# A hybrid decoder layer on eight cores: weights cast to bf16 once and reloaded from a device-memory scratch

## Chip, cores and metric

One Trainium2 chip, all 8 cores. The batch of 16 sequences is split, two sequences per core; the cores run the same program on their own data and do not exchange anything. The metric is the device time in microseconds of the slowest core, taken as the median over several runs.

## The reference

One decoder layer over x of shape (16, 4096, 1024), all in float32:

```python
xn = rms_norm(h, mix_norm)
z = xn @ w_in                               # 3 x 512 conv columns, 3 x 512 q/k/v, 8 forget gates
y_conv = gate_b * causal_depthwise_conv(gate_c * u, conv_w)
y_attn = forgetting_attention(q, k, v, log_sigmoid(z[..., o_f:] + b_f))   # 8 heads x 64, causal
y = group_rms_norm(concatenate([y_conv, y_attn]), mix_out_norm)
h = h + y @ w_o
g, up = split(rms_norm(h, ffn_norm) @ w_gate_up)                          # 2 x 2816
h = h + (silu(g) * up) @ w_down
h = h + sigmoid(rms_norm(h, ple_norm) @ w_ple_gate + b_ple_gate) * (p @ w_ple_proj)
return rms_norm(h, final_norm)
```

The weights are the same for all tokens.

## The kernel before

Each core walks its two sequences in blocks of 512 tokens: 8 blocks a sequence, 16 blocks in all (block 0 to block 15 in this text). A block is computed from end to end before the next: projections and short convolution, attention over all keys of the sequence so far, output projection, feed-forward, the gated input embedding (gate part, L857), final norm. The work grows within a sequence, because attention covers more keys. Activations stay in SBUF as four float32 tiles of 128 tokens (`h_0` to `h_3`), in two sets that alternate from block to block.

Every block streams all weights anew. They are packed on the host into 31 groups (`wpack`, float32) in the order in which a block uses them: 6 for the input projection (0 to 5: q, k, v, b, c, u), 3 for the output projection, then for each of two halves of the feed-forward the gate/up groups (6, then 5) and 4 down groups, 2 for the gate and 1 for the embedding's projection (28 to 30). In bf16 20 of them have 1 MiB, 4 have 0.75, 4 have 0.625 and 3 have 0.5: 27 MiB per block. `issue_group` (L375) loads one group from `wpack` into one of four bf16 slots in SBUF (`wslot`); the transfer is issued on GpSimd's queue (POOL) and casts from float32 to bf16 on the way. `wget` and `wrel` (L394, L399) drive it: group i goes into slot i % 4, and is issued as soon as the program has released group i - 4, that is, behind TensorE's last read of that slot. The first four loads are chained by a buffer `Bchain`: each waits until the one before it has landed.

Everything else that is moved goes on SyncE's queue (SP): the x tiles of the next block at the top of a block (`load_x`, L424), the four p tiles of the block (L751; two buffers, so tiles 2 and 3 wait for the cast of tiles 0 and 1 at L753), and the four y tiles at its end (L890). The x load of a tile waits for the y store of the same tile, since both use the same `h` buffer.

Order on each queue is the program's order; a helper class `Prog` records the operations, derives waits from the buffers that each reads and writes, and emits them per engine. A transfer that waits holds up what stands behind it on its engine.

Other lines that are named below: L477 transposes the normalised tile on TensorE and L484 (VectorE) writes it as `xnT`; L492 is the common projection (input, gate/up); L543 the v projection; L767 to L777 the output projection, added to `h` at L783; L817 the down projection; L836 the transposes of p, copied to `pT` by VectorE at L840, which L863 needs in the same step as L857.

Of the kernel before, what the change touches and what calls it, by code (L numbers as in the profile page):

```python
# [7 lines left out]
BF16 = mybir.dt.bfloat16  # L8
# [137 lines left out]
def block_groups():  # L146
    specs = []

    def wspec(kind, **kw):
        d = dict(kind=kind)  # L150
        d.update(kw)
        specs.append(d)
        return len(specs) - 1

    d = {}
    d["win"] = {nm: wspec("cols", w="w_in", c0=512 * j) for nm, j in
                (("q", 3), ("k", 4), ("v", 5), ("b", 0), ("c", 1), ("u", 2))}
    d["woc"] = wspec("rows", w="w_o", r0=0, n=4, c0=0, ncol=1024)
    d["woa"] = [wspec("rows", w="w_o", r0=512, n=4, c0=512 * dh, ncol=512) for dh in range(2)]
    d["ffn"] = []  # L160
    for (f_lo, f_n) in ((0, 12), (12, 10)):
        gu = [wspec("gu", f0=(f_lo + 2 * j) * 128) for j in range(f_n // 2)]
        dn = []
        n1 = f_n // 2
        for dh in range(2):
            a = wspec("rows", w="w_dn", r0=f_lo * 128, n=n1, c0=512 * dh, ncol=512)
            b = wspec("rows", w="w_dn", r0=(f_lo + n1) * 128, n=f_n - n1, c0=512 * dh, ncol=512)
            dn.append((a, b, n1, f_n - n1))
        d["ffn"].append((f_lo, f_n, gu, dn))
    d["pg"] = [wspec("cols", w="w_pg", c0=512 * dh) for dh in range(2)]  # L170
    d["pp"] = wspec("rows", w="w_pp", r0=0, n=2, c0=0, ncol=1024)
    return specs, d

def group_len(g):
    return g["n"] * g["ncol"] if g["kind"] == "rows" else 4096
# [22 lines left out]
def build(nc, nblk=8, nseq=SEQ_PER_CORE):  # L198
    P = Prog()
    es = ExitStack()  # L200

    def dram(name, shape, kind="ExternalInput"):
        return nc.dram_tensor(name, list(shape), F32, kind=kind).ap()

    x_d = dram("x", [SEQ_PER_CORE, S, D])
    p_d = dram("p", [SEQ_PER_CORE, S, 256])
    bspecs, bplan = block_groups()
    NG = len(bspecs)
    wpack_d = dram("wpack", [NG, 128, 4096])
    wf_d = dram("wf", [128, 64])  # L210
    gpc_d = dram("gpc", [128, 24])
    gconv_d = dram("gconv", [128, 4])
# [14 lines left out]
    y_d = dram("y", [SEQ_PER_CORE, S, D], kind="ExternalOutput")  # L227

    def sb(name, shape, dt):
        return es.enter_context(nc.sbuf_tensor(name, list(shape), dt))  # L230
# [62 lines left out]
    hT = [[sb(f"h{b}_{t}", [128, D], F32) for t in range(4)] for b in range(2)]  # L293
# [40 lines left out]
    pin = [sb(f"pin{i}", [128, 256], F32) for i in range(2)]  # L334
# [5 lines left out]
    NSLOT = 4  # L340
    wslot = [sb(f"wslot{i}", [128, 4096], BF16) for i in range(NSLOT)]
    Bslot = [Buf() for _ in range(NSLOT)]
# [29 lines left out]
    Bchain = Buf()  # L372
    Bchain.w = Bc_pool.w

    def issue_group(i):  # L375
        g = bspecs[i % NG]
        s_ = i % NSLOT
        n = group_len(g)
        o = wslot[s_][:, 0:n]
        i_ = wpack_d[i % NG, :, 0:n]  # L380
        wr = [Bslot[s_], Bchain] if i < NSLOT else [Bslot[s_]]
        P.dma("pool", lambda e, o=o, i_=i_: e.dma_start(out=o, in_=i_), f"w{s_}", writes=wr)  # L382

    released = set()

    def wpump():
        while wstate["issued"] < NGROUPS:
            j = wstate["issued"]
            if j >= NSLOT and (j - NSLOT) not in released:
                break  # L390
            issue_group(j)
            wstate["issued"] += 1
# [19 lines left out]
    for gb in range(nseq * nblk):  # L412
        off = gb * NG
        d = {}
# [9 lines left out]
    def load_x(sq, blk, hb):  # L424
        for tt in range(4):
            r0 = blk * T + tt * 128
            P.dma("sp", lambda e, o=hT[hb][tt][:], i_=x_d[sq, r0:r0 + 128, :]: e.dma_start(out=o, in_=i_),
                  f"h{hb}_{tt}", writes=[Bh[hb][tt]])

    def rstd_all(hb):  # L430
# [68 lines left out]

    gblk = 0  # L500
    load_x(0, 0, 0)
    for sq in range(nseq):
        for blk in range(nblk):
            hb = gblk % 2
# [3 lines left out]
            if nxt < nseq * nblk:  # L508
                load_x(nxt // nblk, nxt % nblk, nxt % 2)
# [8 lines left out]
            for hp in range(4):  # L518
# [4 lines left out]
                     reads=[Bps[b]], writes=[BQT[2 * hp]])  # L523
                P.op("act", lambda e, b=b, hp=hp: e.activation(out=QT[64:128, 2 * hp + 1, :], in_=PS[b][64:128, :],
                                                                func=AF.Copy, scale=0.125),
                     reads=[Bps[b]], writes=[BQT[2 * hp + 1]])
            wrel(pl["win"]["q"])
            sK, BK = wget(pl["win"]["k"])
            for hp in range(4):
# [3 lines left out]
                     reads=[Bps[b]], writes=[BKT[hp]])  # L533
# [55 lines left out]
            def ftr(e, bx=bx, blk=blk):  # L589
                ins = None  # L590
                for tt in range(4):
# [5 lines left out]
                 reads=[Bps[bx]], writes=[Bcrow])  # L597
# [105 lines left out]
            for i in range(len(units) + LOOK):  # L703
                if i < len(units):
                    h, kt, c0, dg, first, last = units[i]
                    hp, s_ = h // 2, h % 2
# [5 lines left out]
                    def fqk(e, sbk=sbk, hp=hp, rows=rows, kt=kt, c0=c0, dg=dg, h=h):  # L712
# [10 lines left out]
                        out=Pb[pi][:, c0:T], in_=PS[sbk][:, c0:T], func=AF.Exp, bias=cK[:, kt, h:h + 1], scale=1.0),  # L723
                        reads=[Bps[sbk], BcK], writes=[BP[pi]])
                j = i - LOOK
                if j >= 0:
                    h, kt, c0, dg, first, last = units[j]
                    if first:
# [5 lines left out]
                        reads=[BP[pi], BVA], writes=[Bps[ob]])  # L734
                    if last:
                        P.op("act", lambda e, ob=ob: e.activation(out=osq[0:65, :], in_=PS[ob][0:65, :],  # L736
                                                                   func=AF.Square),
                             reads=[Bps[ob]], writes=[Bosq])
# [9 lines left out]

            for tt in range(4):
                r0 = q0 + tt * 128  # L750
                P.dma("sp", lambda e, o=pin[tt % 2][:], i_=p_d[sq, r0:r0 + 128, :]: e.dma_start(out=o, in_=i_),  # L751
                      f"pin{tt % 2}", writes=[Bpin[tt % 2]])
                P.op("dve", lambda e, tt=tt: e.tensor_copy(out=pbf[:, tt, :], in_=pin[tt % 2][:]),  # L753
                     reads=[Bpin[tt % 2]], writes=[Bpbf[tt]])
# [4 lines left out]
            for tt in range(4):  # L759
                for dh in range(2):  # L760
# [14 lines left out]
                    def fo2(e, b=b, tt=tt, wav=wav):  # L775
# [8 lines left out]
                        out=hh[:, dh * 512:(dh + 1) * 512], in0=hh[:, dh * 512:(dh + 1) * 512], in1=PS[b][:],  # L784
# [4 lines left out]
            for (f_lo, f_n, gu, dn) in pl["ffn"]:  # L789
                for j in range(f_n):  # L790
# [7 lines left out]
                         reads=[Bps[bg]], writes=[Bsg[si]])  # L798
                    P.op("dve", lambda e, bu=bu, si=si, j=j: e.tensor_tensor(out=actT[:, j, :], in0=sg[si][:],  # L799
                                                                              in1=PS[bu][:], op=ALU.mult),  # L800
                         reads=[Bsg[si], Bps[bu]], writes=[BactT[j]])
                    if j % 2 == 1:
                        wrel(gu[j // 2])
                for dh in range(2):
# [5 lines left out]
                    for tt in range(4):  # L810
                        b = bank()

                        def fd(e, b=b, tt=tt, av=av, bv_=bv_, na=na, nb=nb):
# [9 lines left out]
                            out=hh[:, dh * 512:(dh + 1) * 512], in0=hh[:, dh * 512:(dh + 1) * 512], in1=PS[b][:],  # L823
# [7 lines left out]
            def ftp(e, pbv=pbv):  # L831
                ins = None
                for pc in range(2):
# [7 lines left out]
                 reads=[Bps[tb]], writes=[BpT])  # L841
# [4 lines left out]
            for dh in range(2):  # L846
# [5 lines left out]
                for tt in range(4):  # L852
                    bgt, bpp = bank(), bank()

                    def fg(e, bgt=bgt, bpp=bpp, tt=tt, dh=dh, pgv=pgv, ppv=ppv):
# [6 lines left out]
                        for pc in range(2):  # L862
# [5 lines left out]
                         reads=[Bps[bgt]], writes=[Bacc])  # L868
                    P.op("dve", lambda e, bpp=bpp: e.tensor_tensor(out=acc[:], in0=acc[:], in1=PS[bpp][:],  # L869
                                                                    op=ALU.mult),  # L870
                         reads=[Bps[bpp]], writes=[Bacc])
                    hh = hT[hb][tt]
                    P.op("dve", lambda e, hh=hh, dh=dh: e.tensor_tensor(
                        out=hh[:, dh * 512:(dh + 1) * 512], in0=hh[:, dh * 512:(dh + 1) * 512], in1=acc[:],
# [8 lines left out]
            for tt in range(4):  # L883
                h = hT[hb][tt]
                P.op("dve", lambda e, h=h, tt=tt: e.scalar_tensor_tensor(out=h[:], in0=h[:],
                                                                          scalar=stat[:, 8 + tt:9 + tt],
                                                                          in1=gfin[:], op0=ALU.mult, op1=ALU.mult),
                     reads=[Bstat[tt], Bconst], writes=[Bh[hb][tt]])
                r0 = q0 + tt * 128
                P.dma("sp", lambda e, h=h, o=y_d[sq, r0:r0 + 128, :]: e.dma_start(out=o, in_=h[:]),  # L890
                      f"h{hb}_{tt}", reads=[Bh[hb][tt]])
            gblk += 1

# [70 lines left out]
```

How the kernel before makes its waits and increments, by code:

```python
        def run(engname, eng, final=False):  # L106
            waited = {}
            idx = 0
            for fn, deps, dsem in self.q[engname]:
                for (k, v) in deps:
                    if waited.get(k, 0) < v:
                        eng.wait_ge(sems[k], rank[k][v] if k in rank else v)
                        waited[k] = v
                ins = fn(eng)
                if dsem is None:
                    idx += 1
                    if idx in needed[engname]:
                        ins.then_inc(sems[engname], 1)
                else:
                    ins.then_inc(sems[dsem], 16)
            if final:
                for name, v in self.dma_cnt.items():
                    if waited.get(name, 0) < v:
                        eng.wait_ge(sems[name], v)
```

The softmax here doesn't subtract the row's maximum and nothing guards it: scores larger than these inputs give would overflow.

## Time and profile before

| | us |
|---|---|
| median of 6 runs | 5850.04 (5838.74 to 5922.26) |
| profiled execution, its own time | 5842.04 |
| its span, slowest core (core 6) | 5840.5 |
| spans of the 8 cores | 5821.8 to 5840.5 |
| TensorE matmuls busy | 4991.7 (85%) |
| ScalarE busy | 2552.4 (44%) |
| VectorE busy | 1630.1 (28%) |
| GpSimd busy | 271.9 (5%) |
| device memory read, written (one core) | 950.13 MB, 33.55 MB |

Times are microseconds from the start of the span. PE is TensorE, DVE VectorE, ACT ScalarE, POOL GpSimd, SP SyncE; a q behind the name (SPq) is that engine's issuing of transfers. In rows of a timeline the brackets hold how long the engine was idle before the instruction, and what it had waited for. In rows of the waits the numbers are the total in us, how often, and the longest. In rows of windows each engine has its busy us and its number of instructions, followed by TensorE's granted clock as a share of 2.4 GHz, the mean busy share of the 16 DMA engines, and GB/s counted at the destination.

### The profile page before, as it was taken

To read this page: it belongs to the slowest core of one execution; us is meant where nothing else is said; L and a number is where in the kernel's file an instruction comes from. 1 tells how busy PE (TensorE), PEld (TensorE's weight loads), DVE (VectorE), ACT (ScalarE), POOL (GpSimd) and SP (SyncE) were. 2 spreads that over 40 slices of the span, in tenths; PEclk is the share of its full clock that TensorE was granted. 3 is DMA by queue.
4 is the path that set the end of the run, shared out by engine and by line. 5 is a ranking of instruction groups with operands and counts; after the bars stand their busy time and mean duration, and the time that the engine had idled before them with its cause. 6 is when DMAs were issued, how large, how long until landed. Compare 5 with 4: busy or idle time off the path is not lost.

```text
span 5840.5 us, 76413 instructions; the slowest of 8 cores (5821.8 to 5840.5 us)
## 1 busy us (share of the span) xinstructions
PE 4991.7 (85%) x23664; PEld 2316.0 (40%) x24128; DVE 1630.1 (28%) x2492; ACT 2552.4 (44%) x4663; POOL 271.9 (5%) x509
## 2 busy tenths in 40 slices
PE   5978788898889879889979797888888898888888
PEld 2433334343444334434434343334444344344443
DVE  3242423222240240231242323241312402313113
ACT  3142342625428148258242514336262382572662
POOL 0000000000000000000000000000000000000000
PEclk9989899998999989999989898989999899899999
DMA  5656638174470650840747475572725607417216
GB/s 106 118 110 107 121 60 153 25 133 85 71 143 15 114 114 3 137 89 6 134 94 133 91 120 106 89 139 39 137 53 101 127 3 137 89 29 130 56 34 113
DMA packets 101977, 534.92 MB, mean 92 GB/s; under 512 B 12768, under 2 KB 21344, under 8 KB 60640
## 3 DMA queue, kind: packets, MB, share of 16 engines
q0 software_dynamic: 72720, 453.75, 45.3%
q1 hardware_dynamic: 28880, 76.26, 3.9%
q8 instruction: 222, 3.64, 0.2%
q14 instruction: 155, 1.27, 0.1%
HBM read 950.13 MB, written 33.55 MB: 168 GB/s over the span
## 4 chain that ended last, share of the span: by engine, by line
PE 71%; DVE 12%; ACT 7%; issue 6%; DMA 4%; DVEq 0%; ACTq 0%; POOL 0%; another core or an unknown queue 0%; POOLq 0%
PE ps L492 29%; PE ps L817 9%; PE ps L732 8%; PE ps L715 7%; PE ps L713 7%; DMA wslot<-wpack 4%; DVE xnT L484 3%; PE ps L767 2%; PE ps L771 2%; DVE acc L869 2%; ACT acc L867 1%; PE ps L543 1%; ACT sqb L736 1%; ACT P L722 1%; PE ps L777 1%
## 5 line engine op out<-in xcount | busy, mean ns | idle before, releaser
L492 PE MATMUL ps<-xnT,wslot 128*128 128x512 bf16 x8017 | 1887.7, 396 | 86.6 <-DVE xnT L484 60.7
L722 ACT ACTIVATE P<-ps,cK 128x512 bf16<-128x512 f32 (+3 forms) x2304 | 1341.3, 651 | 92.8 <-PE ps L715 40.2
L492 PEld LDWEIGHTS ps<-xnT,wslot 128*128 128x128 bf16 x8192 | 827.7, 102 | 1127.3 <-issue 248.2
L713 PE MATMUL ps<-QT,KT 128*128 128x512 bf16 (+3 forms) x2210 | 811.1, 367 | 106.0 <-DVE acc L637 101.1
L732 PE MATMUL ps<-P,VA 128*65 128x512 bf16 (+3 forms) x2304 | 840.9, 365 | 45.4 <-ACT P L722 16.0
L715 PE MATMUL ps<-crow,sel_s 128*128 128x512 bf16 (+3 forms) x2258 | 827.0, 366 | 5.2 <-PE ps L732 0.2
L817 PE MATMUL ps<-wslot,actT 128*128 128x512 bf16 x2752 | 609.5, 379 | 50.0 <-DVE actT L799 46.6
L382 POOL DMA_DIRECT2D wslot<-wpack x496 | 266.8, 540 | 5521.0 <-PE ps L492 2147.7
L797 ACT ACTIVATE sqb<-ps 128x512 bf16<-128x512 f32 x176 | 105.2, 598 | 826.7 <-PE ps L492 820.8
L817 PEld LDWEIGHTS ps<-wslot,actT 128*128 128x128 bf16 x2816 | 273.2, 98 | 386.3 <-issue 61.7
L732 PEld LDWEIGHTS ps<-P,VA 128*65 128x65 bf16 x2304 | 252.3, 110 | 430.2 <-issue 360.0
L477 PE MATMUL ps<-identb,xnbf 128*128 128x128 bf16 x1536 | 153.1, 263 | 232.7 <-DVE xnT L484 147.2
L715 PEld LDWEIGHTS ps<-crow,sel_s 128*128 128x128 bf16 x2304 | 227.3, 99 | 246.1 <-issue 14.2
L797 ACT ACTIVATE sg<-ps 128x512 bf16<-128x512 f32 x176 | 105.2, 598 | 488.8 <-PE ps L492 488.8
L713 PEld LDWEIGHTS ps<-QT,KT 128*128 128x128 bf16 x2304 | 227.2, 99 | 207.6 <-issue 122.2
L857 PE MATMUL ps<-wslot,xnT 128*128 128x512 bf16 x992 | 261.3, 407 | 40.4 <-DMA wslot<-wpack 35.0
L799 DVE TENSOR_TENSOR actT<-sqb,ps 128x512 bf16<-128x512 bf16 x176 | 121.1, 688 | 548.9 <-PE ps L492 524.2
L685 DVE SCALAR_TENSOR_TENSOR yTa<-ps,gattn_s,rs 64x512 bf16<-64x512 f32 x64 | 47.5, 743 | 773.6 <-ACT rs L682 773.6
L799 DVE TENSOR_TENSOR actT<-sg,ps 128x512 bf16<-128x512 bf16 x176 | 121.1, 688 | 488.6 <-PE ps L492 488.6
L689 DVE SCALAR_TENSOR_TENSOR ytmp<-ps,gattn_s,rs 64x512 bf16<-64x512 f32 x64 | 47.5, 743 | 716.0 <-ACT rs L682 380.5
L484 DVE TENSOR_TENSOR xnT<-ps,gpc_s 128x1024 bf16<-128x1024 bf16 x192 | 234.6, 1222 | 10.0
L477 PEld LDWEIGHTS ps<-identb,xnbf 128*128 128x128 bf16 x1536 | 120.0, 118 | 270.8 <-issue 267.2
(129 smaller groups left out, 3533.2 us busy)
## 6 DMA issues: line engine op xcount, KB each, us to landing
wslot<-wpack POOLq DMA_DIRECT2D x320, 1024.0 KB, 12.9
wslot<-wpack POOLq DMA_DIRECT2D x64, 768.0 KB, 8.3
wslot<-wpack POOLq DMA_DIRECT2D x64, 640.0 KB, 8.8
wslot<-wpack POOLq DMA_DIRECT2D x48, 512.0 KB, 7.1
h_0<-x SPq DMA_DIRECT2D x16, 512.0 KB, 12.0
h_1<-x SPq DMA_DIRECT2D x16, 512.0 KB, 18.3
h_2<-x SPq DMA_DIRECT2D x16, 512.0 KB, 21.8
h_3<-x SPq DMA_DIRECT2D x16, 512.0 KB, 24.6
```

Source lines behind the costliest of these rows:

```text
L382: P.dma("pool", lambda e, o=o, i_=i_: e.dma_start(out=o, in_=i_), f"w{s_}", writes=wr)
L477: ins = e.transpose(out=pbv[:, kc * 128:(kc + 1) * 128], in_=xb[:, kc * 128:(kc + 1) * 128], identity=identb[:])
L484: P.op("dve", lambda e, pbv=pbv, gb=gb, tt=tt: e.tensor_tensor(out=xnT[:, :, tt * 128:(tt + 1) * 128], in0=pbv.rearrange("p (k t) -> p k t ...
L492: ins = e.matmul(PS[b][:], lhsT=wv[:, kc, c0:c0 + 128], rhs=xnT[:, kc, :], start=(kc == 0), stop=(kc == 7))
L713: e.matmul(PS[sbk][:, c0:T], lhsT=KT[:, hp, kt * 128:(kt + 1) * 128], rhs=QT[:, h, c0:T], start=True, stop=False)
L715: ins = e.matmul(PS[sbk][:, c0:T], lhsT=sel[:, h * 128:(h + 1) * 128], rhs=crow[:, c0:T], start=False, stop=(not dg))
L722: P.op("act", lambda e, sbk=sbk, pi=pi, c0=c0, kt=kt, h=h: e.activation(out=Pb[pi][:, c0:T], in_=PS[sbk][:, c0:T], func=AF.Exp, bias=cK[:, ...
L732: P.op("pe", lambda e, ob=ob, kt=kt, h=h, pi=pi, c0=c0, first=first, last=last: e.matmul(PS[ob][0:65, c0:T], lhsT=VA[:, kt, h, :], rhs=Pb[ ...
L797: P.op("act", lambda e, bg=bg, si=si: e.activation(out=sg[si][:], in_=PS[bg][:], func=AF.Silu), reads=[Bps[bg]], writes=[Bsg[si]])
L799: P.op("dve", lambda e, bu=bu, si=si, j=j: e.tensor_tensor(out=actT[:, j, :], in0=sg[si][:], in1=PS[bu][:], op=ALU.mult), reads=[Bsg[si], ...
L817: ins = e.matmul(PS[b][:], lhsT=actT[:, j, tt * 128:(tt + 1) * 128], rhs=rhs, start=(j == 0), stop=(j == na + nb - 1))
L857: e.matmul(PS[bgt][:], lhsT=xnT[:, kc, tt * 128:(tt + 1) * 128], rhs=pgv[:, kc, :], start=(kc == 0), stop=False)
```

## The change

The first use of each group (block 0) loads it with the cast on GpSimd's queue as before; behind it SyncE's queue stores the bf16 slot to a scratch in device memory, `wscr`, one tensor per core. All later blocks load the group from `wscr`, already bf16, on SyncE's queue. A slot's next load waits for TensorE's reads as before, and in block 0 for the scratch store too. The x loads, p loads and y stores move from SyncE's queue to GpSimd's.

```diff
+    wscr_d = nc.dram_tensor("wscr", [NG, 128, 4096], BF16, kind="Internal").ap()
+    Bscr = [Buf() for _ in range(NG)]
...
     def issue_group(i):
-        g = bspecs[i % NG]
+        gi = i % NG
+        g = bspecs[gi]
         s_ = i % NSLOT
         n = group_len(g)
         o = wslot[s_][:, 0:n]
-        i_ = wpack_d[i % NG, :, 0:n]
-        wr = [Bslot[s_], Bchain] if i < NSLOT else [Bslot[s_]]
-        P.dma("pool", lambda e, o=o, i_=i_: e.dma_start(out=o, in_=i_), f"w{s_}", writes=wr)
+        if i < NG:
+            i_ = wpack_d[gi, :, 0:n]
+            wr = [Bslot[s_], Bchain] if i < NSLOT else [Bslot[s_]]
+            P.dma("pool", lambda e, o=o, i_=i_: e.dma_start(out=o, in_=i_), f"w{s_}", writes=wr)
+            P.dma("sp", lambda e, o=o, d=wscr_d[gi, :, 0:n]: e.dma_start(out=d, in_=o), f"v{s_}",
+                  reads=[Bslot[s_]], writes=[Bscr[gi]])
+        else:
+            P.dma("sp", lambda e, o=o, d=wscr_d[gi, :, 0:n]: e.dma_start(out=o, in_=d), f"u{s_}",
+                  reads=[Bscr[gi]], writes=[Bslot[s_]])
...
-            P.dma("sp", lambda e, o=hT[hb][tt][:], i_=x_d[sq, r0:r0 + 128, :]: e.dma_start(out=o, in_=i_),
+            P.dma("pool", lambda e, o=hT[hb][tt][:], i_=x_d[sq, r0:r0 + 128, :]: e.dma_start(out=o, in_=i_),
                   f"h{hb}_{tt}", writes=[Bh[hb][tt]])
...
-                P.dma("sp", lambda e, o=pin[tt % 2][:], i_=p_d[sq, r0:r0 + 128, :]: e.dma_start(out=o, in_=i_),
+                P.dma("pool", lambda e, o=pin[tt % 2][:], i_=p_d[sq, r0:r0 + 128, :]: e.dma_start(out=o, in_=i_),
                       f"pin{tt % 2}", writes=[Bpin[tt % 2]])
...
-                P.dma("sp", lambda e, h=h, o=y_d[sq, r0:r0 + 128, :]: e.dma_start(out=o, in_=h[:]),
+                P.dma("pool", lambda e, h=h, o=y_d[sq, r0:r0 + 128, :]: e.dma_start(out=o, in_=h[:]),
                       f"h{hb}_{tt}", reads=[Bh[hb][tt]])
```

## Rows read from the trace of the kernel before

**Rows 1.** The page: span, and busy time of each engine.
```profile
span 5840.5 us, 76413 instructions; the slowest of 8 cores (5821.8 to 5840.5 us)
...
PE 4991.7 (85%) x23664; PEld 2316.0 (40%) x24128; DVE 1630.1 (28%) x2492; ACT 2552.4 (44%) x4663; POOL 271.9 (5%) x509
```

**Rows 2.** Table of waits: who waited for whom (us in total, times, longest).
```profile
PE ps L477 <- DVE xnT L484: 147.2, 96, 4.2
...
PE ps L857 <- DMA wslot<-wpack: 35.0, 13, 3.8
...
PE ps L492 <- DMA wslot<-wpack: 7.5, 5, 3.8
...
PE ps L543 <- DMA wslot<-wpack: 1.4, 1, 1.4
```

**Rows 3.** TensorE's timeline in blocks 0, 1 and 15 (start, us, instructions).
```profile
77.74 7.07 PE L492 MATMUL ps<-xnT,wslot 128*128 128x512 bf16 x31 [3.83 <-DMA wslot<-wpack]
...
240.47 34.69 PE L492 MATMUL ps<-xnT,wslot 128*128 128x512 bf16 x157 [0.71 <-DMA wslot<-wpack]
...
306.14 3.19 PE L857 MATMUL ps<-wslot,xnT 128*128 128x512 bf16 x7 [3.59 <-DMA wslot<-wpack]
...
612.92 1.01 PE L836 MATMUL ps<-identb,pbf 128*128 128x128 bf16 x8 [0.32 <-DVE xnT L484]
617.75 3.19 PE L857 MATMUL ps<-wslot,xnT 128*128 128x512 bf16 x7 [3.82 <-DMA wslot<-wpack]
...
621.98 1.89 PE L857 MATMUL ps<-wslot,xnT 128*128 128x512 bf16 x8
...
5803.31 3.19 PE L857 MATMUL ps<-wslot,xnT 128*128 128x512 bf16 x7 [1.54 <-DVE pT L840]
```

**Rows 4.** The page's DMA queues: packets, MB, share (software_dynamic is GpSimd's, hardware_dynamic SP's).
```profile
q0 software_dynamic: 72720, 453.75, 45.3%
q1 hardware_dynamic: 28880, 76.26, 3.9%
```

**Rows 5.** Windows: start of block 0, its feed-forward, a gate/up stretch; two of block 1.
```profile
33.00:78.00 45.00, 33.62 (x172) 15.89 (x175) 10.19 (x24) 7.60 (x18) 3.19 (x6) 0.96 0.76 127
...
164.00:306.00 142.00, 123.91 (x591) 57.85 (x603) 43.78 (x58) 28.25 (x54) 11.84 (x22) 0.93 0.80 136
...
240.00:276.00 36.00, 34.53 (x157) 15.57 (x160) 7.51 (x11) 5.98 (x10) 3.47 (x7) 1.00 0.97 165
...
606.00:616.00 10.00, 4.25 (x40) 3.25 (x40) 9.58 (x12) 6.62 (x15) 1.02 (x2) 0.61 0.98 159
...
649.00:661.00 12.00, 12.00 (x49) 5.08 (x48) 4.39 (x6) 4.74 (x8) 0.53 (x1) 0.85 0.97 250
```

**Rows 6.** GpSimd's timeline in block 0: weight loads as they are issued.
```profile
44.61 0.53 POOL L382 DMA_DIRECT2D wslot<-wpack  x1 [10.15 <-DMA wslot<-wpack]
54.22 1.59 POOL L382 DMA_DIRECT2D wslot<-wpack  x3 [9.08 <-DMA wslot<-wpack]
...
164.61 1.69 POOL L382 DMA_DIRECT2D wslot<-wpack  x3 [63.37 <-PE ps L777]
...
190.34 0.53 POOL L382 DMA_DIRECT2D wslot<-wpack  x1 [6.38 <-PE ps L492]
```

**Rows 7.** The chain that ended last: load of group 5 (start, us).
```profile
55.26 22.35 DMA wslot<-wpack
```

**Rows 8.** SyncE's timeline: issue of the last y store.
```profile
5836.96 0.33 SPq L890 DMA_DIRECT2D y<-h_3  x1
```

**Rows 9.** DMA issues: two constants, KB each, us to landing.
```profile
identf<-ident SPq DMA_DIRECT2D x1, 64.0 KB, 1.8
...
identb<-ident POOLq DMA_DIRECT2D x1, 32.0 KB, 3.2
```

**Rows 10.** VectorE's timeline behind attention in block 2: the cast of p, first addition.
```profile
792.82 0.29 DVE L753 CAST pbf<-pin 128x256 bf16<-128x256 f32 x1 [0.28 <-DMA pin<-p]
...
794.82 0.69 DVE L783 TENSOR_TENSOR h_0<-h_0,ps 128x512 f32<-128x512 f32 x1 [1.70 <-PE ps L777]
```

## The prediction

> **What bounds the kernel now.** Read the page's busy shares first: TensorE is busy 85% of a span of 5840.5 us, no other engine above 44% [rows 1]. TensorE is what the end hangs on, so this change is worth what TensorE waits for weights, and no more. The table of waits gives that directly: TensorE waited on a weight transfer 35.0 us ahead of the gate projection (L857, 13 times), 7.5 us ahead of L492 (5 times) and 1.4 us ahead of L543 (once), 43.9 us in all, or 0.75% of the span. Beside that, one wait of another kind, for the normalised tile of L484, costs 147.2 us and is not touched [rows 2]. Half of the weight bytes could go and still no more than 44 us could be won there.
>
> The PE timeline says where these waits lie. In block 1 the transposes of L836 end at 613.93, and the gate matmuls start only at 617.75, 3.82 us idle for a weight load. In block 15 the same place waits only 1.54 us, and for pT (DVE L840), not for weights [rows 3]. That is the next thing late: a wait removed at L857 leaves about 1.54 us standing.
>
> The third view is the DMA's share. From 164 to 306 us (feed-forward part of block 0) the 16 DMA engines are busy 0.80 of the time; in the gate/up stretch 240 to 276 it is 0.97 at 165 GB/s [rows 5]. The DMA engines are nearly full in exactly the stage in which, in block 0, the change adds work.
>
> **Prices of a transfer.** A casting load moves 165 GB/s (counted at the bf16 end) at 0.97 busy, 170 at full, so 1 MiB of bf16 takes 6.2 us of all DMA engines; the whole run says the same, 453.75 MB in 45.3% of 5840.5 us, 171 GB/s [rows 4, 5]. Plain transfers on SP's queue (x, p, y) moved 76.26 MB in 3.9%, 335 GB/s, so 1 MiB takes 3.1 us [rows 4]. A scratch store or a reload of bf16 without a cast is in neither queue of this trace; x and y are the nearest rows, and I take 3.1 us for both. A mixed stretch bears out that the two kinds add up in one set of engines: 649 to 661 us, y stores beside weight loads, moved 250 GB/s, between 170 and 335 [rows 5].
>
> **Blocks 1 to 15: what goes.** A block's 31 groups (27 MiB) take 27 x 6.2 = 167 us of DMA time now and 27 x 3.1 = 84 us after, but only awaited time counts. Of the 13 waits of L857 one (3.59 us) is block 0's [rows 3]; the other 12 sum to 35.0 - 3.6 = 31.4 us, and 12 x 1.54 = 18.5 us of that stays as the wait for pT. Gain 12.9 us. Of L492's 7.5 us, 3.83 and 0.71 belong to block 0 [rows 3]; the other three, 3.0 us, go. Together -15.9 us.
>
> The order of issue is kept: weights stay the only traffic on their queue after block 0, and a reload is issued at the same release of a slot as now. The wait it adds, on its scratch store, has been met a whole block earlier.
>
> **Blocks 0 to 15: the activations' move.** Each block issues 4 x loads, 4 p loads and 4 y stores on GpSimd instead of SP, 12 per block. GpSimd takes 0.53 us for an issue [rows 6]; from block 1 on it has nothing else to do. What stood behind a waiting SP instruction now stands behind the same one on GpSimd: p tiles 2 and 3 wait for the cast of tiles 0 and 1, y stores for the final multiply, x loads for the y store of the same tile. x is needed a block later, so it is covered. p tiles 2 and 3 are issued at the end of attention and VectorE waits for them now; after the last cast it idled 1.70 us for TensorE [rows 10]. A 32 KB constant on GpSimd's queue landed after 3.2 us, a 64 KB one on SP's after 1.8 us [rows 9]; 1.4 us more is inside those 1.70 us, so nothing. If the cover went, each us late would cost at most 16 us. In block 0 the p loads stand ahead of weight groups 10 to 12, but wait only until 145 us, and these groups start at 164.61 [rows 6]. The last y store was issued 3.5 us ahead of the end [rows 8] and is on the path: +1.5 us for the other queue.
>
> **Block 0: what is added.** Every weight group is loaded with the cast as before, then SP stores it to scratch, 27 MiB, at s = 3.1 us a MiB. The slot's next load must also wait for that store, and loads share the DMA engines with stores. Two places have no room:
>
> (a) Start. The first loads are chained, each on the last: groups 2 and 3 are issued at 44.61 and 54.22 as the one before has landed, the last together with groups 4 and 5 [rows 6]; group 5 landed at 77.61 [rows 7], and TensorE stood waiting for it 3.83 us [rows 3]. Stores of groups 0 to 3 (the last partly) now fall among these loads: 3.6 x 3.1 = 11.2 us later. The engines are idle a quarter of this stretch (0.76 busy [rows 5]), but as the latency of chained loads, which a store does not fill. The x loads only change queue here, at the same bytes.
>
> (b) Feed-forward and gate part, 164 to 306 us. Loads of groups 10 to 30, 18 MiB, are 18 x 6.2 = 112 us; the row says 0.80 x 142 = 114, so 28 us are free, of which some 3 are the first load's latency: 25 usable [rows 5]. Stores of groups 10 to 27, 15.5 MiB, want 15.5 x 3.1 = 48 us. 48 - 25 = 23 us more than fits. A gate/up group lasts 6.91 us on TensorE (its release comes 6.38 us after a 0.53 us issue [rows 6]) against 6.2 + 3.1 = 9.3 us on the DMA engines: four slots hide the first few, then TensorE goes at their pace, and the last group lands 23 us later, where TensorE waits already [rows 3].
>
> So block 0 costs 3.6 s + 15.5 s - 25 = 19.1 s - 25 = 34 us at s = 3.1. Bounds of s: 0, if stores run in time that loads leave unused inside the engines (block 0 then costs nothing), and 6.2, the casting load's price, which makes 93 us.
>
> **Sum**, against the profiled execution's 5842.0 us: -15.9 + 1.5 + 34 = +19.6, 5861.6 us. The median of six runs, 5850.0, stands 8 us above that execution, half of the runs at 5839 to 5841, so it may or may not carry over: I add half, 4, and give 5865.
>
> **Rivals.**
> 1. Stores cost nothing (s under 1.3): the reads of HBM are what is slow in a casting load, and stores slip beside them. Then only -15.9 + 1.5 remains: 5828, with the 4 us 5832. For it: DMA engines idle 20% of 164 to 306. Against: 0.97 in the middle of it [rows 5], and 250 GB/s in the mixed stretch lies between the two rates instead of at their sum.
> 2. Slower, by the store's price: writing 1 MiB to device memory while eight cores load costs what the casting load costs, s = 6.2. Block 0 loses 93 us: +79, 5921, with the 4 us 5925. It is slower by over 1% from s = 5.1 on (19.1 x 5.1 - 25 - 14 = 58). Against: y stores are part of the 335 GB/s [rows 4].
> 3. The activations become late on GpSimd: p tiles 2 and 3 land 5 us later in each block, 3.3 us past the cover, 16 x 3.3 = 53 us: 5918. Against: the 1.4 us between two constants [rows 9].
> 4. The shorter gap spares TensorE the slow restart: seven matmuls took 3.19 us at L857, eight later 1.89, after a stretch granted 0.61, between the levels of 1.2 and 2.4 GHz [rows 3, 5]. 15 x 1.3 = 20 us more won: 5845. Against: block 15, with 1.54 us of waiting, starts with the same 3.19 us.
>
> Rival 3 has a rule beside it. The Trainium skill (SBUF — State Buffer, "SBUF: two separate sides") says that a transfer issued from GpSimd stalls while VectorE runs an operation that takes both port pairs, since GpSimd can't write its descriptors then; moving x, p and y there would expose them, and would free the weights of it. No row here shows such a stall apart. By this rule the weights would gain, but were awaited 44 us only; p tiles 2 and 3 go out between two short casts, and would lose less than the cover.
>
> **How the numbers follow.** Forecast 0.57 (own range 5846 to 5885, s from 2 to 4), rival 1 0.20, rival 2 0.13, rival 3 0.05, rival 4 0.05. The range 5824 to 5915 takes in rivals 1 and 4 and s up to about 4.9. A measurement of this kernel tells about 1% (58 us) from no change: over 1% slower needs rival 2, rival 3 or a harder block 0, 0.14; over 1% faster would need more than all TensorE's waits for weights, 0.03; within 1%, 0.83.
>
> **What would show it.** Right: TensorE's wait for weights near 0 from block 1 on, L857 waiting about 1.5 us for pT; the gate part of block 0 beginning some 30 us after 306, with the DMA engines busy without a break from 164; DMA's share in later gate/up stretches near half; VectorE not later at the first L783. Wrong: block 0 as long as before (rival 1) or 60 us longer (rival 2); VectorE waiting for p past TensorE (rival 3); fast first matmuls at L857 (rival 4). What would refute the whole sum is a matmul, a cast or an exponential that itself takes another time than before.

## The result, and the profile after

The changed kernel takes 5891.3 us (median of 10 runs) against 5844.0 us for the kernel before in the same series (median of 20): ratio 1.0084, 95% interval 1.0055 to 1.0113. In some executions the cores of one die (0 to 3 or 4 to 7), or of both, show a lower granted clock and take longer, so ratios, intervals and single times in this text are of executions without that, and where one die alone was free of it, only its cores are used. The changed kernel is some 47 (medians) to 49 us (ratio) slower. That lies in the range on record and just inside the 1% that I called no change; the forecast value, 5865, was 26 us short. Its profiled execution took 5889.1 us (before: 5842.0), its slowest core 5887.6 us.

The time can be split at one instruction, the first final multiply of a block (L885 before, L894 after: `h_0` times `gfin_s`). Its first occurrence ends block 0, its last one is in block 15. VectorE's timeline on core 6, the slowest core before, in the kernel before:

```profile
336.30 1.28 DVE L885 SCALAR_TENSOR_TENSOR h_0<-h_0,stat,gfin_s 128x1024 f32<-128x1024 f32 x1
...
5832.01 1.28 DVE L885 SCALAR_TENSOR_TENSOR h_0<-h_0,stat,gfin_s 128x1024 f32<-128x1024 f32 x1 [5.15 <-ACT stat L438]
```

and the same core in the changed kernel:

```profile
387.14 1.28 DVE L894 SCALAR_TENSOR_TENSOR h_0<-h_0,stat,gfin_s 128x1024 f32<-128x1024 f32 x1
...
5873.70 1.28 DVE L894 SCALAR_TENSOR_TENSOR h_0<-h_0,stat,gfin_s 128x1024 f32<-128x1024 f32 x1 [5.15 <-ACT stat L447]
```

Block 0 ends 50.8 us later. Blocks 1 to 15 take 5873.70 - 387.14 = 5486.6 us instead of 5495.7: 9.1 us less. From that last occurrence to this core's end at 5886.4 it takes 12.7 us, instead of 8.5: 4.2 us more. Together +45.9 us, the difference of this core's spans. The forecast had the same three terms as +34, -15.9 and +1.5.

The table of waits, TensorE's rows on core 6 of the changed kernel (answer to [rows 2]):

```profile
PE ps L501 <- DMA wslot<-wpack: 23.5, 8, 5.2
PE ps L866 <- DVE pT L849: 23.4, 15, 1.7
PE ps L826 <- DMA wslot<-wpack: 16.0, 3, 7.7
PE ps L866 <- DMA wslot<-wpack: 8.1, 1, 8.1
PE ps L552 <- DMA wslot<-wpack: 3.8, 1, 3.8
```

All remaining waits for weights are for casting loads (`wpack`), which only block 0 issues; no row names the scratch. From block 1 on TensorE waits for no weights. In their place at L866 (L857 before) stands pT, 15 times, 1.56 us each. But block 0 alone now waits 23.5 + 16.0 + 8.1 + 3.8 = 51.4 us for weights, more than the whole kernel did. Where, is seen in TensorE's timeline of block 0, core 6 (answer to [rows 3]). The first matmuls of the feed-forward part before:

```profile
173.91 43.51 PE L492 MATMUL ps<-xnT,wslot 128*128 128x512 bf16 x188 [2.02 <-DVE xnT L484]
```

and block 0 of the changed kernel:

```profile
91.99 2.72 PE L501 MATMUL ps<-xnT,wslot 128*128 128x512 bf16 x6 [5.19 <-DMA wslot<-wpack]
...
189.83 36.22 PE L501 MATMUL ps<-xnT,wslot 128*128 128x512 bf16 x156 [2.02 <-DVE xnT L493]
...
243.67 3.57 PE L826 MATMUL ps<-wslot,actT 128*128 128x512 bf16 x8 [7.73 <-DMA wslot<-wpack]
...
320.89 1.01 PE L826 MATMUL ps<-wslot,actT 128*128 128x512 bf16 x2 [6.54 <-DMA wslot<-wpack]
...
357.93 2.89 PE L866 MATMUL ps<-wslot,xnT 128*128 128x512 bf16 x7 [8.11 <-DMA wslot<-wpack]
```

Group 5, which let TensorE go on at 77.74 us before, comes at 91.99: 14.3 us later (forecast 11.2). The feed-forward part's first matmuls start at 189.83 instead of 173.91, 15.9 us later; the gate part starts at 357.93 instead of 306.14, 51.8 us later. So all that lies ahead of the feed-forward part costs 15.9 us, where 11.2 were forecast, and the feed-forward part 35.9, where 23 were forecast. The windows of that core (answer to [rows 5]) show the DMA engines full in both places; the last two numbers are their busy share and GB/s:

```profile
62.00:100.00 38.00, 26.57 (x122) 12.03 (x124) 7.71 (x23) 3.18 (x11) 1.57 (x3) 0.76 0.98 214
...
180.00:359.00 179.00, 133.02 (x593) 59.36 (x606) 43.81 (x58) 28.25 (x54) 11.16 (x21) 0.88 0.97 210
...
602.00:638.00 36.00, 35.17 (x161) 15.83 (x162) 7.44 (x11) 5.98 (x10) 0.00 (x0) 1.00 0.39 143
```

The third row is the second gate/up stretch of block 1, with reloads: 0.39 busy at 143 GB/s, where the same stretch of block 0 before had 0.97 at 165 GB/s [rows 5]. GpSimd's timeline on the same core shows that the slot's wait for its store holds back loads too; the last row is from the table of waits:

```profile
206.31 0.53 POOL L386 DMA_DIRECT2D wslot<-wpack  x1 [6.92 <-DMA wscr<-wslot]
215.62 0.53 POOL L386 DMA_DIRECT2D wslot<-wpack  x1 [8.79 <-PE ps L501]
224.98 0.53 POOL L386 DMA_DIRECT2D wslot<-wpack  x1 [8.83 <-DMA wscr<-wslot]
233.38 0.53 POOL L386 DMA_DIRECT2D wslot<-wpack  x1 [7.87 <-DMA wscr<-wslot]
...
POOL wslot L386 <- DMA wscr<-wslot: 62.8, 8, 10.5
```

A load was issued every 6.91 us before [rows 6]; here it is every 8.4 to 9.4 us. Three of the four rows shown were released by a store's landing (`wscr<-wslot`), not by TensorE; over the whole kernel it is eight loads, all in this part of block 0.

### The profile page after: what moved, and what is told of

It is laid out like the page before. It is cut to its first block, busy times and chain, and to the rows that moved or that the text cites. A ratio compares the mean times of both kernels' runs of the same rounds, so it can differ in the third digit from the quotient of the medians.

```text
span 5887.6 us, 76970 instructions; the slowest of 8 cores (5871.8 to 5887.6 us)
## 1 busy us (share of the span) xinstructions
PE 5067.4 (86%) x24128; PEld 2322.7 (39%) x24128; DVE 1627.5 (28%) x2492; ACT 2549.5 (43%) x4663; POOL 123.9 (2%) x236
## 4 chain that ended last, share of the span: by engine, by line
PE 69%; DVE 13%; ACT 8%; issue 5%; DMA 4%; DVEq 0%; ACTq 0%; POOL 0%; POOLq 0%; SPq 0%
PE ps L501 28%; PE ps L826 8%; PE ps L741 8%; PE ps L722 7%; PE ps L724 7%; DVE xnT L493 4%; DMA wslot<-wpack 3%; PE ps L776 2%; PE ps L780 2%; DVE acc L878 1%; PE ps L552 1%; ACT acc L876 1%; PE ps L866 1%; ACT sqb L745 1%; ACT P L731 1%
## 5 line engine op out<-in xcount | busy, mean ns | idle before, releaser
L501 PE MATMUL ps<-xnT,wslot 128*128 128x512 bf16 x8192 | 1920.4, 399 | 79.2 <-DVE xnT L493 52.6
L722 PE MATMUL ps<-QT,KT 128*128 128x512 bf16 (+3 forms) x2304 | 847.2, 368 | 101.8 <-DVE acc L646 101.8
L724 PE MATMUL ps<-crow,sel_s 128*128 128x512 bf16 (+3 forms) x2304 | 846.8, 368 | 0.0
L724 PEld LDWEIGHTS ps<-crow,sel_s 128*128 128x128 bf16 x2304 | 227.3, 99 | 246.3 <-issue 14.4
L866 PE MATMUL ps<-wslot,xnT 128*128 128x512 bf16 x1024 | 271.6, 413 | 26.3 <-DVE pT L849 17.7
L453 ACT ACTIVATE junk<-h_0 128x1024 bf16<-128x1024 f32 x33 | 34.9, 1057 | 339.8 <-DVE h_0 L831 237.2
## 6 DMA issues: line engine op xcount, KB each, us to landing
wscr<-wslot SPq DMA_DIRECT2D x20, 1024.0 KB, 14.4
```

Source lines behind the costliest of these rows:

```text
L501: ins = e.matmul(PS[b][:], lhsT=wv[:, kc, c0:c0 + 128], rhs=xnT[:, kc, :], start=(kc == 0), stop=(kc == 7))
L722: e.matmul(PS[sbk][:, c0:T], lhsT=KT[:, hp, kt * 128:(kt + 1) * 128], rhs=QT[:, h, c0:T], start=True, stop=False)
L724: ins = e.matmul(PS[sbk][:, c0:T], lhsT=sel[:, h * 128:(h + 1) * 128], rhs=crow[:, c0:T], start=False, stop=(not dg))
L866: e.matmul(PS[bgt][:], lhsT=xnT[:, kc, tt * 128:(tt + 1) * 128], rhs=pgv[:, kc, :], start=(kc == 0), stop=False)
```

## The experiments

Two theories of block 0. A: the stores take time of DMA engines that are nearly full. B: the slot waits for its store, and the next load comes late. Since the end of block 0 differs by up to 19 us between the cores of one execution, I compare its mean over cores; all numbers are VectorE's first and last final multiply, as above. "Rest" is blocks 1 to 15. Each row is one profiled execution.

| kernel | end of block 0, mean (lowest to highest), us | rest, us | time, us |
|---|---|---|---|
| before | 332.8 (328.2 to 337.0) | 5484.1 to 5495.7 | 5842.0 |
| changed | 383.9 (375.0 to 389.7) | 5481.7 to 5486.6 | 5889.1 |
| no_reload | 381.0 (371.0 to 390.3) | 5483.4 to 5494.9 | 5895.5 |
| small_store | 332.8 (326.7 to 337.6) | 5483.9 to 5492.4 | 5840.3 |
| free_slot | 373.2 (361.4 to 379.9) | 5473.0 to 5490.9 | 5877.2 |
| double_store (cores 0 to 3) | 448.8 (443.9 to 453.2) | 5483.0 to 5484.7 | |
| spare_start | 368.0 (358.6 to 376.7) | 5489.9 to 5494.6 | 5882.4 |
| act_only | 332.0 (327.2 to 337.9) | 5484.0 to 5491.4 | 5843.4 |
| weights_again | 379.8 (372.1 to 385.9) | 5481.4 to 5486.8 | 5880.9 |
| spread_again (cores 0 to 3) | 330.4 (325.8 to 335.0) | 5490.5 to 5491.2 | |

A finer measure splits block 0: from its first feed-forward matmul to its first gate matmul (173.91 and 306.14 us above) the mean over cores is 130.7 us before, 165.6 in the changed kernel, 165.2 in no_reload, 164.8 in weights_again and 165.4 in spare_start. So executions with the same stores and waits there agree within 0.8 us.

**no_reload: the stores alone.**

```diff
-            P.dma("sp", ... e.dma_start(out=o, in_=d), f"u{s_}", reads=[Bscr[gi]], ...
+            P.dma("pool", ... e.dma_start(out=o, in_=i_), f"w{s_}", writes=[Bslot[s_]])   # i_: wpack_d
```

(x, p and y are on SyncE's queue here, as before.)

> The kernel before, plus the stores of the changed one: every weight group is stored to scratch in block 0, but all later blocks go on loading with the cast on GpSimd's queue, and x, p and y stay on SyncE's. Both theories expect block 0 as long as in the changed kernel, its first final multiply (L894 there) some 50 to 60 us later than before (336 us on core 6), and so 5893 to 5903 us in all, against 5842 before. It tells what the reloads themselves win: if blocks 1 to 15 take 5495 us on the slowest core as before, against some 5486 with reloads, the reloads are worth 9 us; if they take 5486 here too, the reloads are worth nothing.

Measured: ratio to before 1.0076 (1.0038 to 1.0114), the profiled execution 5895.5 us. Block 0 ends at 381.0 us on the mean, 48.2 us later than before. So the stores in block 0 make the whole loss. Its slowest core took 5494.9 us for the rest, 8 to 13 us more than any core of the changed kernel, but the other seven 5483.4 to 5487.2, no more than those with reloads. So in these executions the reloads win some 9 us on the slowest core, and next to nothing on the others. That is not firmly shown: the ratios of whole runs (1.0076 here, 1.0084 with reloads) are too wide for it, and in free_slot, which has no reloads either, the rest takes as little as 5473.0 us on one core, for a reason that stays open.

**small_store: the wait without the bytes.**

```diff
-  lambda e, o=o, d=wscr_d[gi, :, 0:n]: e.dma_start(out=d, in_=o)
+  lambda e, o=wslot[s_][:, 0:n // 8], d=wscr_d[gi, :, 0:n // 8]: e.dma_start(out=d, in_=o)
```

> As no_reload, but only the first eighth of each row of a group is stored, and the slot's next load still waits for that store. Theory A (the stores' time on the DMA engines, some 4 us per MiB): 0.5 us per MiB fits in what is free, block 0 within 10 us of before, 5842 to 5854 us in all. Theory B (the wait of a slot for its store): the wait is still there, behind a store that is as late in its queue; block 0 at least 25 us longer, 5867 us or more. The scratch is not read by anything.

Measured: 5840.3 us, block 0 at 332.8 us, no later than before. A wait for a store that is short costs nothing here. The window of 164 to 306 us on core 4 shows the engines a little fuller than core 6 in [rows 5] (0.80), and no more:

```profile
164.00:306.00 142.00, 125.56 (x598) 58.18 (x608) 44.43 (x59) 28.88 (x58) 11.67 (x22) 0.94 0.86 150
```

So a wait alone is not enough; this leaves open what the wait does when the store is long.

**free_slot: the bytes without the wait.**

```diff
+    dump = sb("dump", [128, 2048], BF16)                # zeros
...
-  reads=[Bslot[s_]], writes=[Bscr[gi]])
+  Bland = Buf(); Bland.w = Bslot[s_].w                  # wait for the load, do not hold the slot
+  P.dma_multi("sp", [... e.dma_start(out=d, in_=dump[:, 0:m]) ...], f"v{s_}", reads=[Bland, Bdump], ...)
```

> As no_reload, but what is stored comes from a constant tile of zeros of the same total size, once the group's load has landed: as many bytes are written, and no load waits for a store. What is written to scratch is not the weights, and nothing reads it. Theory A: block 0 stays 45 to 60 us longer than before, 5885 to 5903 us in all. Theory B: with the wait gone block 0 is within 15 us of before, 5842 to 5858 us.

Measured: 5877.2 us, block 0 at 373.2 us, 40.4 us later than before: near A's range, below it, and far from B's. The bytes make most of the loss. Against no_reload, which differs from it by the wait, 7.8 us are missing on the mean, and they lie in the feed-forward part: 157.5 us from its first matmul to the gate part, against 165.2, while that part begins at the same time (185.7 and 185.8 us). The stores of the two also differ in form (halves of a row, from a tile of zeros), which no run takes apart from the wait; if the form costs nothing, some 8 us are the wait's. GpSimd's timeline on core 6 shows loads of a gate/up stretch issued at TensorE's pace again, 6.91 us apart, and the window shows the engines full all the same:

```profile
204.81 0.53 POOL L389 DMA_DIRECT2D wslot<-wpack  x1 [6.38 <-PE ps L507]
211.72 0.53 POOL L389 DMA_DIRECT2D wslot<-wpack  x1 [6.38 <-PE ps L507]
...
190.00:320.00 130.00, 111.17 (x478) 48.17 (x477) 22.48 (x33) 14.42 (x23) 7.91 (x15) 0.92 1.02 200
```

What the wait changes is seen in the DMA issues. Without it a store of 0.5 MB lands 27.4 us after its issue (median), so stores fall behind and end beside later work; with it a store of 1 MB lands after 14.4 us. The wait forces stores to keep up with loads. DMA issues of free_slot on core 6 and, in the second fence, of the changed kernel's page (core 1):

```profile
wscr<-dump SPq DMA_DIRECT2D x51, 512.0 KB, 27.4
```

```profile
wslot<-wscr SPq DMA_DIRECT2D x300, 1024.0 KB, 6.6
...
wscr<-wslot SPq DMA_DIRECT2D x20, 1024.0 KB, 14.4
```

**double_store: the price of a store.**

```diff
+  P.dma("sp", lambda e, o=o, d=wscr2_d[gi, :, 0:n]: e.dma_start(out=d, in_=o), f"vv{s_}",
+        reads=[Bslot[s_]], writes=[Bscr2[gi]])
```

> The changed kernel with every group stored twice in block 0, to two scratches. Theory A: 27 MiB more at s us per MiB, of which 19.1 MiB lie on the path; with the s of 3.9 to 4.1 that the changed kernel's block 0 asks for, block 0 grows by another 75 to 78 us, to some 465 us at its first final multiply, 5963 to 5969 us in all; at 3.1 it would grow by 59. Theory B: the second store lands shortly after the first, so the wait grows by a store's own time alone, under 30 us in all, 5890 to 5920 us.

Measured, on cores 0 to 3: block 0 at 448.8 us against 384.5 for the same four cores of the changed kernel, 64.3 us more. That is twice what B allowed at most, and less than A's 75 to 78; the spans are 5941 to 5949 us, under A's 5963. If no free time is left and the same 19.1 MiB count, all of the second set costs: 64.3 / 19.1 = 3.4 us per MiB, an estimate. So s is about 3.4, above the 3.1 that I took and under the 3.9 that I had read out of the changed kernel's block 0. (By places: 55.1 us for the 15.5 MiB of the feed-forward part, 3.6 each, and 9.8 us for the 3.6 MiB ahead of it, 2.7 each.) In a stretch of it on core 0, with one load and two stores per group, the DMA share is 1.03 and the engines move 228 GB/s: full, while TensorE is busy for only 24.82 of 40 us:

```profile
260.00:300.00 40.00, 24.82 (x99) 10.39 (x100) 5.11 (x8) 0.00 (x0) 2.12 (x4) 0.79 1.03 228
```

Here too the slot waits for both stores, so this run alone does not separate bytes from wait. But the DMA queues give the same price without a second store. Core 6, 164 to 306 us before (first row) and 180 to 359 us in the changed kernel (packets, MB, share of the 16 engines):

```profile
q0 software_dynamic: 3071, 19.26, 80.1%
```

```profile
q0 software_dynamic: 3024, 18.88, 70.3%
q1 hardware_dynamic: 2941, 18.61, 25.9%
```

Before, loads took 0.801 x 142 = 113.7 us for 18.4 MiB, 6.2 us per MiB. Beside stores they took 0.703 x 179 = 125.8 us for 18.0 MiB, 7.0 per MiB. The stores themselves took 0.259 x 179 = 46.4 us for 17.7 MiB, only 2.6 per MiB. With the 0.8 us that each MiB of loads takes longer, 14.4 us in all, a MiB of stores costs 60.8 / 17.7 = 3.4 us. So a good part of a store's price stands in the loads beside it. Whether the engines or the device memory that eight cores share make those packets longer, no run here separates.

**spare_start: the start apart from the feed-forward part.**

```diff
-        if i < NG:
+        if i < NG or (gi < 6 and i < 2 * NG):
...
+            if i >= (NG if gi < 6 else 0):          # the store
```

> The changed kernel with groups 0 to 5 (the input projection) loaded with the cast once more in block 1 and stored there, so that block 0's start has no stores. The prediction's two places in block 0 then come apart: the start's share (14.7 to 16 us by the changed kernel's timeline, group 5 landing 14.7 us later and the feed-forward part beginning 15.8 us later) goes, and the feed-forward's 37 us stay: block 0 ends 32 to 42 us later than before instead of 44 to 59, and block 1 pays at most 5 us for the six stores, which lie beside attention and the input projection: 5872 to 5880 us. If block 0 stays at 375 to 390 us, the start was not on the path.

Measured: 5882.4 us; block 0 ends at 368.0 us, 15.9 us earlier than in the changed kernel and 35.2 us later than before. The two places come apart as expected: the feed-forward part begins at 172.4 us on the mean, against 171.7 before and 188.0 in the changed kernel, and its 165.4 us stay. The time missed its range by 2 us, since block 1 pays more than 5 us: it takes 319.0 us on the mean against 309.3, and the rest 5492.9 against 5484.3.

**act_only and weights_only: the two parts of the change.** act_only moves x, p and y in the kernel before (the edit shown); weights_only leaves them on SyncE's queue in the changed one (the same edit backwards), and weights_again is the same kernel as weights_only.

```diff
-  P.dma("sp", ...)      # x loads, p loads, y stores
+  P.dma("pool", ...)
```

> The kernel before with x, p and y moved to GpSimd's queue, behind and between the weight loads. If the move is free by itself: 5842 us within 6 us, and blocks 1 to 15 on the slowest core 5490 to 5500 us. If activations on GpSimd's queue are late (p tiles 2 and 3, or a weight load that stands behind an x load that waits for a y store), each block is some us longer: 5860 us or more.

> The changed kernel with x, p and y back on SyncE's queue, between the reloads. If the activations' move is free, this is the changed kernel again: 5882 to 5894 us, block 0 ending at 375 to 390 us. If the reloads need a queue of their own (a reload of group 4 stands behind x loads that wait for y stores), blocks 1 to 15 are longer: 5900 us or more. If the activations' move cost time, this one is faster by it: under 5878 us.

> The same kernel as weights_only, whose profile was disturbed; its one undisturbed time was 5881.7 us. If the activations' move is free: 5878 to 5892 us, blocks 1 to 15 within 5483 to 5488 us on all cores, block 0 ending at 375 to 390 us.

Measured: act_only 1.0010 (0.9997 to 1.0023) of before, block 0 and the rest as before. weights_only took 5881.7 us; weights_again 5880.9 us, block 0 at 379.8 us, the rest as with the full change. So the move costs nothing that shows in blocks 1 to 15, nor in block 0 without stores. With stores block 0 ends 4.1 us earlier with x and p on SyncE's queue (379.8 against 383.9), most of it ahead of the feed-forward part (184.8 against 188.0); one execution each can't tell that from nothing. The move costs at the end: core 0 of weights_again ends 8.5 us after its last final multiply, as before, where the changed kernel takes 12.7 and act_only 12.5 us.

**spread: the stores where the engines are free.** The scratch is filled over blocks 0 to 5.

```diff
+    sblk = {6: 0, 7: 0, 8: 0, 9: 0}
+    for k, gi in enumerate([g for g in range(NG) if g not in sblk]):
+        sblk[gi] = 1 + k % 5
...
-        if i < NG:
+        if i // NG <= sblk[gi]:
...
+            if i // NG == sblk[gi]:                  # the store, on SyncE's queue
...
+            P.dma("pool", ... e.dma_start(out=o, in_=d), f"w{s_}", ...)   # the reload
```

> The scratch is filled over six blocks: in block 0 only groups 6 to 9 are stored (they sit in their slots through attention), the other 27 groups in blocks 1 to 5, every fifth group in each; a group is loaded with the cast up to the block in which it is stored, and reloaded as bf16 behind it. All weights go on GpSimd's queue, scratch stores and x, p, y on SyncE's. Theory A (the stores' time on full DMA engines in block 0 is the loss): five or six MiB of stores a block, 17 to 22 us, fit into the 28 us that the engines have free in a block's feed-forward part, block 0 ends within 3 us of before, and from block 6 on the reloads win what they win: 5833 to 5843 us, ratio 0.998 to 1.000. If the cost is the store itself wherever it stands, the total stays near the changed kernel's, 5880 to 5892 us.

> The same kernel as spread, for an interval. On a die that nothing disturbed it took 5832 to 5838 us there, against 5830 to 5842 for the kernel before. Theory A: ratio 0.998 to 1.001, block 0 within 3 us of before. It would be a gain that can be told from nothing only under 0.997.

Measured: the first series gave one time, 5837.8 us, and no interval; the second gave 0.9997 (0.9982 to 1.0011) of the kernel before, and block 0 ends at 330.4 us on the mean, no later than before (333.1 on the same cores). In the feed-forward part of block 1 on core 2 the engines have room for the stores: 0.87 busy, where the same window before had 0.83.

```profile
490.00:610.00 120.00, 112.69 (x523) 50.10 (x522) 27.26 (x40) 19.91 (x37) 10.10 (x19) 1.00 0.87 155
```

The same stores cost 50 us in block 0, and some 6 us when spread (the rest takes 5490.8 us on the mean, against 5484.3 in the changed kernel), most of it in blocks 1 and 2. That is about what the reloads win on the slowest core, so this version gives back the whole loss but does not beat the kernel before.

## Why the prediction was right or wrong

**The bound.** Right. What reloads could win was bounded by TensorE's waits for weights, less what pT would leave at the same place. From block 1 on the waits for weights are gone, and pT stands at L866, 15 times 1.56 us, against 1.54 forecast.

**Blocks 1 to 15: -15.9 forecast, -9.1 measured on core 6.** The waits fell as worked out: L857 and L492 lost 31.4 + 3.0 us, pT came back with 23.4 - 4.6 = 18.8, which makes 15.6. Yet the blocks became only 9.1 us shorter. The windows of blocks 1 to 15 on core 6, before and after, show what went against it:

```profile
336.30:5832.01 5495.71, 4748.41 (x22482) 2201.55 (x22924) 1513.68 (x2320) 2453.84 (x4467) 248.10 (x461) 0.92 0.49 90
```

```profile
387.14:5873.70 5486.56, 4764.35 (x22482) 2207.36 (x22924) 1512.18 (x2321) 2454.25 (x4467) 94.31 (x176) 0.92 0.25 90
```

TensorE was idle 25.1 us less (722.2 instead of 747.3), but busy 15.9 us longer with the same 22482 matmuls (their ends are modelled in these rows, so both sizes are rough). The prediction had let every wait that goes shorten the block, with matmuls as long as before. Block 3 shows one such place, before and after:

```profile
1298.17 3.17 PE L857 MATMUL ps<-wslot,xnT 128*128 128x512 bf16 x7 [2.62 <-DMA wslot<-wpack]
...
1301.39 0.59 PE L863 MATMUL ps<-wslot,pT 128*128 128x512 bf16 x2
```

```profile
1346.01 3.19 PE L866 MATMUL ps<-wslot,xnT 128*128 128x512 bf16 x7 [1.54 <-DVE pT L849]
...
1349.42 1.00 PE L872 MATMUL ps<-wslot,pT 128*128 128x512 bf16 x2
```

Block 3 begins at 979.24 us before and at 1027.27 after. The gate matmuls start 0.19 us earlier in the block, but the first L872 (L863 before) comes at the same 322.15 us of it and then takes 1.00 us instead of 0.59; the stretch behind the transposes of L836 (L845) and the wait is granted 0.50, the 1.2 GHz level, in both. So TensorE began sooner and stayed slow for more of its matmuls. That this makes all of the 15.9 us was not added up block by block.

The term also differs by core. Cores 0 and 2 became 7.3 and 9.9 us shorter, but core 1 took 5484.1 us before and 5485.0 after, since it waited for weights only 4.6 us in the whole kernel. Nor is it always the same core: the longest rest without reloads is core 6's in the kernel before, core 2's in no_reload, core 4's in small_store and core 0's in act_only. The kernel's time is its slowest core's, so the most that reloads could win is what set that core apart from the others.

**Block 0: 34 forecast, 50.8 measured on core 6 (51.1 on the mean).** The mechanism, full DMA engines at the start and in the feed-forward part, was right, and rival 1 (stores for nothing) and rival 2 (a store as dear as a casting load) are out: double_store and the DMA queues put s at about 3.4. Two sizes were off in part (b), the feed-forward part, with 34.9 us on the mean instead of 23. One is s: 3.4 instead of 3.1 makes 15.5 x 0.3 = 5 us. The other is the step "25 usable". With s = 3.4, 15.5 x 3.4 = 53 us were to be placed there. Without the slot's wait (free_slot) 27 of them showed, so 26 us were absorbed, near the 25 forecast, though partly because stores ended beside later work. With the wait 35 showed, so only 18 were. I had written that the slot's next load waits for the store, and then counted as if the engines could fill every gap. How the 12 us divide hangs on s: with 3.6, from the feed-forward part of double_store alone, the price makes 7 of them. Part (a), the start, 11.2 forecast, took 15.9; the price makes 1 us of that difference, the rest was not explained.

**The tail: +1.5 forecast, +4.2 measured.** The last y store is issued 7.3 us ahead of core 6's end, against 3.5 [rows 8]. GpSimd's timeline:

```profile
5879.13 0.53 POOL L899 DMA_DIRECT2D y<-h_3  x1 [0.66 <-DVE h_3 L894]
```

The issue itself comes 1.84 us after its multiply has started (5877.29), 1.35 before; the rest is from issue to the end. The prediction had taken its 1.5 us from two small constants [rows 9].

**The activations inside the blocks.** Right at nothing. VectorE's timeline behind attention in block 2 of core 6 (answer to [rows 10]) shows the cover shrink from 1.70 to 0.76 us and hold. The cast of p tile 2 before:

```profile
792.25 0.29 DVE L753 CAST pbf<-pin 128x256 bf16<-128x256 f32 x1 [1.95 <-DMA pin<-p]
```

and the rows of the changed kernel:

```profile
842.16 0.29 DVE L762 CAST pbf<-pin 128x256 bf16<-128x256 f32 x1 [2.79 <-DMA pin<-p]
842.83 0.29 DVE L762 CAST pbf<-pin 128x256 bf16<-128x256 f32 x1 [0.37 <-DMA pin<-p]
843.88 0.69 DVE L792 TENSOR_TENSOR h_0<-h_0,ps 128x512 f32<-128x512 f32 x1 [0.76 <-PE ps L786]
```

Over the whole kernel VectorE on core 6 waited 50.5 us for p with p on GpSimd's queue (changed, and act_only) and 37.5 and 38.7 with p on SyncE's (before, and weights_again): some 0.4 us more for each of about 32 waits, inside the cover. Rival 3 is out, by act_only too. The Trainium skill's rule beside it (SBUF — State Buffer, "SBUF: two separate sides"), that VectorE can keep GpSimd from writing descriptors, would have made x, p and y late; in these rows all that could be its doing is the 0.4 us, and no run tells it from the queue's own time. Rival 4 is out as priced: in block 1 of core 6 the first seven gate matmuls still took 3.19 us after a wait of 1.62.

```profile
666.30 3.19 PE L866 MATMUL ps<-wslot,xnT 128*128 128x512 bf16 x7 [1.62 <-DVE pT L849]
```

**The range and chances.** 5824 to 5915 holds 5891; the likeliest case's own range, 5846 to 5885, does not, and it had a chance of 0.57. The three terms were all off to the slow side, by 17, 7 and 3 us on core 6, so none made up for another. The prediction's "s up to about 4.9" for the range does not follow from its sum: s = 4.9 gives some 5900 us, and 5915 belongs to 5.7. The measured value lies inside the 1%, near its edge.

## What to carry to other kernels

Preparing data once is not free because it happens once: here 27 MiB of stores in one block whose DMA engines were already nearly full cost over five times what fifteen blocks of cheaper loads won on core 6, and the same stores spread over six blocks cost about what the loads won. Count free time of a shared resource only as far as the waits let it be used: a buffer that is held until its copy has landed can waste as much of it as the copy needs. And read a saving on every core: a wait that only some cores have is worth at most the distance to the others, and less where the matmuls behind it run at a lower clock.

## What the runs showed that I had not expected

With y on GpSimd's queue the end of the kernel came 7.3 us after the last y store's issue, with y on SyncE's 3.5 us, for the same 512 KB. In blocks 4 to 15 the changed kernel's cores 1 and 6 agree in each block's length to 0.13 us, although they carry different data, while core 6 before differs from them by up to 2.7 us in a block (392.3 against 389.6 in block 13).
